# The last expert's up projection ahead of three of its neighbour's down pieces; list slots by position; weights spread by GpSimd; lists read back by a gather

## What is computed

```python
logits = xt @ w_router + b_router
top_vals, top_idx = lax.top_k(logits, 4)            # 32 experts, 4 of them for a token
top_gates = softmax(top_vals)
# for each expert e, on its rows xb:
gate = minimum(xb @ w_gate[e] + b_gate[e], 7)
up = clip(xb @ w_up[e] + b_up[e], -7, 7)
y = (gate * sigmoid(1.702 * gate) * (up + 1)) @ w_down[e] + b_down[e]
out[token] += top_gates[token, e] * y               # summed over the token's experts
```

## Time and profile before

| | |
|---|---|
| three runs, median (lowest to highest) | 1674.03 us (1672.72 to 1676.4) |
| the profiled execution | 1675.01 us |
| its span in the trace | 1673.7 us |
| TensorE busy | 1609.6 us (96%) |
| VectorE busy | 1351.4 us (81%) |
| ScalarE busy | 1194.3 us (71%) |
| GpSimd busy | 239.6 us (14%) |
| chain that ended last | PE 76%, DVE 13%, ACT 6%, issue 3%, DMA 1% |

### The profile page before, as it was taken

One profiled execution on the slowest core, in us unless ns is written; L12 is line 12 of the kernel. 1 busy time (PEld: TensorE's weight loads), 2 busy tenths in 40 slices (PEclk: granted clock), 3 DMA queues, 4 the chain that ended last, 5 costly groups with the idle time before them and its releaser, 6 DMA issues.

```text
span 1673.7 us, 19532 instructions
## 1 busy us (share of the span) xinstructions
PE 1609.6 (96%) x7495; PEld 1301.5 (78%) x7495; DVE 1351.4 (81%) x1059; ACT 1194.3 (71%) x932; POOL 239.6 (14%) x170
## 2 busy tenths in 40 slices
PE   8999979999999999999999999999999999999998
PEld 6877867777877877877877877877776887788886
DVE  4576689999999999999999999999997535864343
ACT  5354358888888888888898898898894366763232
POOL 2502037131121121121111111112010000000000
PEclk9999989999999999999999999999999999999999
DMA  8412379999999999999999999999994512114311
GB/s 295 136 51 76 124 278 334 406 404 415 414 406 417 411 409 415 408 413 408 410 416 403 411 412 406 410 412 399 403 395 134 188 64 76 51 57 176 101 63 51
DMA packets 97343, 487.86 MB, mean 291 GB/s; under 512 B 14645, under 2 KB 16365, under 8 KB 48096
## 3 DMA queue, kind: packets, MB, share of 16 engines
q1 hardware_dynamic: 82848, 463.69, 69.4%
q0 software_dynamic: 10480, 18.17, 4.2%
q10 hardware_dynamic: 3920, 4.72, 0.8%
HBM read 478.00 MB, written 25.08 MB: 301 GB/s over the span
## 4 chain that ended last, share of the span: by engine, by line
PE 76%; DVE 13%; ACT 6%; issue 3%; DMA 1%; DVEq 0%; ACTq 0%
PE PS L574 68%; ACT WH L1129 5%; DVE WL L1503 4%; DVE low L1503 4%; PE PS L835 3%; PE PS L1050 1%; DVE eu L1865 1%; DVE eu L1870 1%; PE PS L849 1%; PE PS L606 1%; DVE hl L1856 1%; DMA h2d<-HV 1%; PE PS L1064 1%; PE PS L705 0%; PE PS L1043 0%
## 5 line engine op out<-in xcount | busy, mean ns | idle before, releaser
L1129 ACT ACTIVATE WH<-land 128x2048 fp32r<-128x2048 f32 x210 | 396.5, 1912 | 134.6 <-PE PS L574 134.0
L1129 ACT ACTIVATE WH<-ring 128x2048 fp32r<-128x2048 f32 x216 | 407.7, 1912 | 87.3 <-PE PS L574 82.9
L1503 DVE TENSOR_TENSOR low<-ring,WH 128x2048 fp32r<-128x2048 f32 x194 | 437.1, 2287 | 19.5 <-ACT WH L1129 18.6
L1503 DVE TENSOR_TENSOR WL<-land,WH 128x2048 fp32r<-128x2048 f32 x190 | 427.5, 2287 | 20.4 <-ACT WH L1129 19.6
L2223 POOL DMA_INDIRECT accd<-ys,lists x28 | 60.2, 2149 | 742.6 <-ACT ys L1337 734.0
L574 PE MATMUL PS<-WH,xh 128*128 128x512 f32 x512 | 161.0, 396 | 4.1 <-DVE low L1503 1.9
L574 PE MATMUL PS<-WH,hh 128*128 128x512 f32 x512 | 147.4, 389 | 0.0
L574 PE MATMUL PS<-WH,xs 128*128 128x512 f32 x512 | 144.4, 405 | 1.8 <-DVE xs L1854 1.8
L574 PE MATMUL PS<-WH,xl 128*128 128x512 f32 x512 | 137.2, 390 | 0.0
L574 PEld LDWEIGHTS PS<-WH,xs 128*128 128x128 f32 x512 | 98.1, 195 | 22.0 <-issue 2.2
L574 PE MATMUL PS<-h,WH 128*128 128x512 f32 x288 | 113.4, 394 | 0.0
(11 more groups left out here) (443 smaller groups left out, 2975.8 us busy)
## 6 DMA issues: line engine op xcount, KB each, us to landing
land<-in_w_up_dram SPq DMA_DIRECT2D x71, 1024.0 KB, 9.8
ring<-in_w_down_dram SPq DMA_DIRECT2D x71, 1024.0 KB, 10.6
ring<-in_w_gate_dram SPq DMA_DIRECT2D x66, 1024.0 KB, 10.7
land<-in_w_gate_dram SPq DMA_DIRECT2D x62, 1024.0 KB, 11.2
ring<-in_w_up_dram SPq DMA_DIRECT2D x57, 1024.0 KB, 10.2
land<-in_w_down_dram SPq DMA_DIRECT2D x57, 1024.0 KB, 10.8
ring<-in_w_in_dram SPq DMA_DIRECT2D x19, 1024.0 KB, 13.0
land<-in_w_in_dram SPq DMA_DIRECT2D x13, 1024.0 KB, 5.4
```

The lines of the kernel that those rows point to most:

```text
L1129: A.activation(WH[buf[n]], lands[spot[n]], ACT.Copy).then_inc(s_hi, 1)
L1503: V.tensor_tensor(WLn[n], lands[spot[n]], WH[buf[n]].bitcast(F32), SUB).then_inc(s_lo, 1)
```

## The change

- *Last expert.* In stage 31 the order of pieces is `d0 g6 g7 d1 d2 d3` at the end in place of `d0 g6 d1 g7 d2 d3`. The fold of expert 31's up part moves from behind d3 to behind d1, the clamp and product to ahead of the third low half, the transposes from behind d3 to behind d2; their result goes into `xh` instead of `hh`. The bias half and the matmuls of `tensor_hold` between them go; the bias half stands in the join, whose order changes.
- *Slots.* A slot is now position times 32 plus expert, made by one step from the position `P1`; the bit steps go, and two short steps stand in the routing. The lists are read back by one indirect gather, with row numbers `laid`.
- *Weights.* `spread_out` goes; `gpsimd_spread`, three element-wise steps on GpSimd, stands between the first and the second gather there. `vector_further_count` moves behind `vector_last`.
- *Expert 0 and 1.* ScalarE's and VectorE's copies of expert 1's rows move by one piece; `scalar_out(0)` moves from g0 to g4 of stage 2.
- *Warm-up.* One, one and six more matmuls behind the routing's parts, and eleven instead of eight ahead of expert 0.

```diff
@@ -249,4 +251,2 @@
     pvk = reg("pvk", [128, 4, E, K], F32, 17)
-    ri = reg("ri", [128, 4, E], I32, 50)
-    bits = [reg(f"bits{i}", [128, 4, E], I32, (48, 48.5, 50.5, 51)[i]) for i in range(4)]
     WH += [reg(f"WH{3 + i}", [128, 4, 512], F32R, 53.5 + 16 * i) for i in range(2)]
@@ -342,3 +342,4 @@
             return [("d", p) for p in range(4)]
-        return [(a[0], int(a[1])) for a in "g0 g1 g2 g3 g4 g5 d0 g6 d1 g7 d2 d3".split()]
+        row = "g0 g1 g2 g3 g4 g5 d0 g6 d1 g7 d2 d3" if e + 1 < E else "g0 g1 g2 g3 g4 g5 d0 g6 g7 d1 d2 d3"
+        return [(a[0], int(a[1])) for a in row.split()]
 
@@ -477,9 +478,2 @@
 
-    def spread_out(o, v):
-
-        V.tensor_tensor(e2, eq, v.unsqueeze(2).broadcast_to([128, 4, E, K]), MUL).then_inc(dv.sem, dv.one())
-        V.wait_ge(dv.sem, dv.n)
-        return V.tensor_reduce(o, e2, AX, ADD)
-
-
     s_land = s_ring + [s_gpre, s_glog, s_gt, s_wz, s_wgh]
@@ -806,3 +800,5 @@
         tensor_route(1)
+        tensor_stay_warm(1)
         turn2(2)
+        tensor_stay_warm(1)
         turn2(3)
@@ -810,2 +806,4 @@
         tensor_route(3)
+        P.wait_ge(s_tall, 16)
+        tensor_stay_warm(6)
         P.wait_ge(s_m16, 1)
@@ -938,3 +936,3 @@
                 P.wait_ge(s_spk, 1)
-        rows_by_columns(n_d[e, p], p, 4, hh, hl, 0 if p else t_mid[e] + 1, small(e)).then_inc(s_mm, 1)
+        rows_by_columns(n_d[e, p], p, 4, hh if e + 1 < E else xh, hl, 0 if p else t_mid[e] + 1, small(e)).then_inc(s_mm, 1)
         if p == 0 and small(e + 1):
@@ -944,5 +942,7 @@
             tensor_turn_rows(e + 2)
-        if p == 3 and small(e + 1):
+        if p == (3 if e + 2 < E else 1) and small(e + 1):
             P.wait_ge(s_low, fold["up", e + 1])
             tensor_fold(2, eul).then_inc(s_fold, 1)
+        if p == 2 and e + 2 == E:
+            tensor_turn_mid(E - 1)
 
@@ -951,3 +951,3 @@
         tensor_index(0, 7)
-        tensor_stay_warm(8)
+        tensor_stay_warm(11)
         tensor_turn_rows(0)
@@ -957,6 +957,2 @@
                 tensor_down_bias(0)
-                tensor_hold(6, 3)
-                tensor_turn_mid(E - 1)
-                tensor_down_bias(1, (0,))
-                tensor_hold(3, 3)
             for what, p in items(e):
@@ -975,8 +971,2 @@
 
-    def tensor_hold(bank, times):
-        P.wait_ge(s_lo, n_d[E - 1, 0] + 1)
-        P.wait_ge(s_tl, t_rows[E - 1] + 1)
-        for _ in range(times):
-            mm(PS[:, bank, :], foldw, WH[buf[n_d[E - 1, 0]]][:, 0], True, True)
-
     def tensor_last(j, part, end):
@@ -996,3 +986,3 @@
     def tensor_join():
-        tensor_down_bias(1, (1,))
+        tensor_down_bias(1, (0,))
         P.wait_ge(s_last, 3)
@@ -1000,5 +990,6 @@
         tensor_last(0, yh, False)
-        tensor_last(1, yh, False)
+        tensor_down_bias(1, (1,))
         P.wait_ge(s_last, 4)
         tensor_last(0, yl, True)
+        tensor_last(1, yh, False)
         tensor_last(1, yl, True)
@@ -1345,3 +1336,2 @@
                 scalar_out(E - 2)
-                scalar_turn8(t_mid[E - 1], hh, E - 1)
             for what, p in items(e):
@@ -1353,6 +1343,12 @@
                     scalar_rows(e + 1)
-                if (what, p) == ("d", 2) and small(e):
+                if (what, p) == ("d", 2 if e + 1 < E else 1) and small(e):
                     scalar_up_low(e)
+                if (e, what, p) == (E - 1, "d", 3):
+                    scalar_turn8(t_mid[E - 1], xh, E - 1)
+                if (what, p) == ("g", 7) and e == 0:
+                    scalar_rows(1)
+                    A.wait_ge(s_spt, 1)
+                    A.activation(GtT, PS[0:32, 5, :].rearrange("p (j t) -> p j t", j=4), ACT.Copy).then_inc(s_spk, 1)
                 high(ahead(n_g[e, p] if what == "g" else n_d[e - 1, p]))
-                if (what, p) == ("g", 2 if small(e) else 0) and e >= 2:
+                if (what, p) == ("g", 2 if small(e) else 4 if e == 2 else 0) and e >= 2:
                     scalar_out(e - 2)
@@ -1362,6 +1358,2 @@
                     scalar_gate(e)
-                if (what, p) == ("g", 7) and e == 0:
-                    scalar_rows(1)
-                    A.wait_ge(s_spt, 1)
-                    A.activation(GtT, PS[0:32, 5, :].rearrange("p (j t) -> p j t", j=4), ACT.Copy).then_inc(s_spk, 1)
         high(second + 1)
@@ -1714,2 +1706,5 @@
                     low(first)
+                    V.tensor_scalar(chosen[:, :, :, 0], C[:, TOKK:TOKK + 16].rearrange("p (j k) -> p j k", j=4), -1.0, None, ADD).then_inc(dv.sem, dv.one())
+                    V.wait_ge(dv.sem, dv.n)
+                    V.tensor_scalar(chosen[:, :, :, 0], chosen[:, :, :, 0], 2, None, ALU.arith_shift_right)
         invert(8, 7)
@@ -1799,6 +1794,4 @@
         step = lambda o: o.then_inc(dv.sem, dv.one())
-        step(V.tensor_scalar(ri, P1, -1.0, None, ADD))
         V.wait_ge(s_ek, 1)
         step(V.reciprocal(sm, sm))
-        step(V.tensor_scalar(chosen[:, :, :, 0], C[:, TOKK:TOKK + 16].rearrange("p (j k) -> p j k", j=4), -1.0, None, ADD))
         step(V.tensor_tensor(past, P1, late[:, OVT:OVT + 96].rearrange("p (e j) -> p e j", j=3)[:, :, 0].unsqueeze(1).broadcast_to([128, 4, E]), ALU.is_gt))
@@ -1806,11 +1799,6 @@
         V.tensor_tensor(GK, GK, sm.unsqueeze(2).broadcast_to([128, 4, 4]), MUL).then_inc(s_gk, 1)
-        step(V.tensor_scalar(bits[0], ri, 7, None, ALU.bitwise_and))
-        step(V.tensor_scalar(bits[1], ri, 8, None, ALU.bitwise_and))
-        step(V.tensor_scalar(bits[2], ri, 48, None, ALU.bitwise_and))
-        step(V.tensor_scalar(bits[3], ri, 64, None, ALU.bitwise_and))
         step(V.scalar_tensor_tensor(pv, past, 8 * BIG, C[:, IOTA:IOTA + E].unsqueeze(1).broadcast_to([128, 4, E]), MUL, ADD))
         V.wait_ge(dv.sem, dv.n)
-        for b, times in ((0, 128.0), (1, 256.0), (2, 2.0), (3, 16.0)):
-            step(V.scalar_tensor_tensor(pv, bits[b], times, pv, MUL, ADD))
-            V.wait_ge(dv.sem, dv.n)
+        step(V.scalar_tensor_tensor(pv, P1, 1.0 * E, pv, MUL, ADD))
+        V.wait_ge(dv.sem, dv.n)
         step(V.tensor_tensor(pvk, eqr, pv.unsqueeze(3).broadcast_to([128, 4, E, K]), MUL))
@@ -1818,3 +1806,2 @@
         step(V.tensor_reduce(slots, pvk.rearrange("p j e k -> p j k e"), AX, ADD))
-        step(V.tensor_scalar(chosen[:, :, :, 0], chosen[:, :, :, 0], 2, None, ALU.arith_shift_right))
         V.wait_ge(s_gk, 1)
@@ -1822,3 +1809,3 @@
         V.wait_ge(dv.sem, dv.n)
-        V.tensor_copy(sloti, slots).then_inc(s_sig, 1)
+        V.tensor_scalar(sloti, slots, -1.0 * E, None, ADD).then_inc(s_sig, 1)
 
@@ -1898,14 +1885,14 @@
         low(first + NX - 1)
-        spread_out(Gt, GK).then_inc(s_sp, 1)
-        vector_further_count()
         for e in range(E + 1):
             if e == E:
-                vector_turn8(t_mid[E - 1], hh, hl, E - 1)
                 vector_last()
+                vector_further_count()
             for what, p in items(e):
-                if (what, p) == (("d", 1) if e else ("g", 7)) and e + 1 < E:
+                if (what, p) == (("d", 1) if e else ("g", 6)) and e + 1 < E:
                     vector_turn8(t_rows[e + 1], xs if small(e + 1) else xh, xl, e + 1)
-                if (e, what, p) == (E - 1, "d", 3):
+                if (e, what, p) == (E - 1, "d", 2):
                     vector_up(E - 1)
                     vector_glu(E - 1)
+                if (e, what, p) == (E - 1, "d", 3):
+                    vector_turn8(t_mid[E - 1], xh, hl, E - 1)
                 low(ahead(n_g[e, p] if what == "g" else n_d[e - 1, p]))
@@ -2205,5 +2192,14 @@
 
+    def gpsimd_spread():
+        G.wait_ge(s_gk, 1)
+        G.tensor_tensor(e2, eq, GK.unsqueeze(2).broadcast_to([128, 4, E, K]), MUL).then_inc(po.sem, po.one())
+        G.wait_ge(po.sem, po.n)
+        G.tensor_tensor(e2[:, :, :, 0:2], e2[:, :, :, 0:2], e2[:, :, :, 2:4], ADD).then_inc(po.sem, po.one())
+        G.wait_ge(po.sem, po.n)
+        G.tensor_tensor(Gt, e2[:, :, :, 0], e2[:, :, :, 1], ADD).then_inc(s_sp, 1)
+
     def gpsimd_lists():
         G.wait_ge(s_small, 400)
-        G.dma_start(lists.rearrange("p s a -> p (s a)"), listd.rearrange("(p s) a -> p (s a)", s=E)).then_inc(s_small, 16)
+        G.indirect_dma_start(lists.rearrange("p s a -> p (s a)"), None, listd.rearrange("(p s) a -> p (s a)", s=E),
+                             bass.IndirectOffsetOnAxis(laid, 0), bounds_check=127, oob_is_err=False).then_inc(s_small, 16)
         G.wait_ge(s_small, 416)
@@ -2248,6 +2244,9 @@
         gpsimd_gather(1)
+        gpsimd_spread()
         gpsimd_gather(2)
         G.wait_ge(s_sig, 3)
+        G.tensor_copy(laid, C[:, LAID:LAID + 1]).then_inc(po.sem, po.one())
         G.wait_ge(s_small, 144)
         gpsimd_list(0, 16)
+        G.wait_ge(po.sem, po.n)
         gpsimd_lists()
```

(4 more changed lines are left out.)

## The result

Over 20 runs each the changed kernel took **1679.15 us** (1671.39 to 1683.14), the kernel before 1674.89 us (1672.26 to 1676.69): ratio **1.0018**, 95% interval 1.001 to 1.0026, slower by 4.3 us by the medians (3.0 us by the ratio). The forecast of 1678.8 us is 0.35 us off, and inside its range. But its parts are not right: in the profiles the start gained where a loss was forecast, the end lost more, and the join, forecast at nothing, lost most.

The account below looks back on a forecast made before the run. TensorE and VectorE bound the middle, so only the ends could move the time, VectorE bounding the start. Profiled 1675.01 us plus 2.0, 1.1 and 1.7 gave 1679.8, less 1.0 for the median: 1678.8, range 1671.2 to 1681.8.

Parts of the forecast that it names:

- Start: Start of the experts, up to expert 0's GLU product: ends 2.0 us later, bounds -4.1 to +3.0.
- the cost of the spread on GpSimd: Start: GpSimd's last spread step waits for VectorE's row of five low halves; weights known at 254.2 instead of 248.0.
- Rival A: Start: GpSimd's third step slips in between low halves; about -3.5 us at the GLU product; chance 0.31 in three forms.
- The warm-ups: Added TensorE matmuls ahead of the experts: up to 1.5 us later there, nothing in the sum while VectorE is the bound.
- Slots and counts: VectorE, start: shorter slots gain 1.8 us; spread and counts leaving gain 2.30, the counts moving about 1 us at no cost.
- Last expert: TensorE: expert 31's down part starts 1.1 us later, bounds -1 to +2; a slow clock adds 1.7 us.
- The wait: TensorE runs dry for 3.3 us ahead of the last expert's transposes; expert 31's down part starts 1.1 us later.
- The half clock: TensorE behind the last expert's wait: clock at 0.50 over 3 to 4 us of work, +1.7 us; 0 if it holds.
- The join: The order of bias and list steps in the join only fills a gap of 0.3; nothing in the sum.

Follow-up runs that it names:

- spread late: The changed kernel with GpSimd's three spread steps behind the second gather instead of ahead of it; 1682.93 us, ratio 1.0048.
- spread on VectorE: The changed kernel with last expert and join as before, and the weights' spread back on VectorE, none on GpSimd; 1672.70 us, ratio 0.9988.
- wait filled: The changed kernel with twelve unused matmuls in TensorE's wait ahead of the last expert's transposes; 1672.74 us, ratio 0.9996.
- end alone: The kernel before with only the last expert's new order and the new join; 1677.28 us, ratio 1.0023.
- old join: The changed kernel with the join's order as before; 1676.10 us, ratio 1.0008.
- GLU earlier: The changed kernel with the last expert's clamp and product one low half earlier on VectorE; 1670.63 us, ratio 0.9973.
- join filled: GLU earlier with five unused matmuls ahead of the join's first transposes; 1669.76 us, ratio 0.9975.

## Why the prediction was right in its sum and wrong in its steps

- **Start, forecast +2.0, measured -2.4** at the GLU product. The step that failed is the cost of the spread on GpSimd, in two places. It was put behind low half +4 by adding the old duration of one step to the old time of the gather. The gather came 0.87 us earlier, and, what decides, the steps held up VectorE's `pvk` by 1.64 us and with it +4, so they were all over by then. And a step that does meet the row waits for one low half, not for all of them (spread late). Rival A, the open seam, had the sign of the start right (-3.5 forecast for it, -2.4 measured, of which 0.87 is the earlier gather), but in the changed kernel no step needed a seam. The warm-ups, at nothing in the sum, stay unsettled.
- **The Trainium skill's rule** (SBUF — State Buffer, Who interferes with whom): contention between a two-input VectorE instruction and a GpSimd instruction that reads SBUF is in the traces here, as `pvk` at 2.33 instead of 0.69 us. The same section says that issue order decides who blocks; in the records `pvk` starts 0.70 us ahead of GpSimd's step and is the one that is held. As it lasts 0.69 us alone, it would have been over just when that step starts; so these records don't show which of the two was issued first, and neither bear the rule out nor refute it.
- **Slots and counts, forecast 1.8 us and (of the 2.30) some 1.0**: right. With the spread on VectorE the GLU product ends 29.13 us after the first gather starts (268.95 and 239.82), before 31.87: 2.74 us.
- **Last expert, forecast +1.1 and +1.7, measured +3.74** from fold to down. The wait (3.3 forecast, 3.06 measured) and its own price (1.1 forecast, 1.02 with the wait filled) are right. The half clock was mis-sized for this profile: 2.7 us instead of 1.7, as it covered the transposes and the whole piece behind them, up to about 1260. It is not one size: behind the same wait it cost 2.7 and 2.6 in the two profiles of the changed kernel, 1.6 in those of the end alone and of spread late, and nothing in that of the old join.
- **The join, forecast at nothing, measured +4.17** in the profiled execution. This term was missing: the prediction asked of the join's new order only what gap it fills, and not what TensorE's clock does there. It was at half for 7 us in the kernel before and for 17 in the changed one. By the mean clocks a time this long comes in nine of 20 runs. Of the kernels with the wait unfilled, those with the new join have runs above 1679 us (ten of 20 and three of three of the changed kernel, five of twelve of the end alone, four of six of spread late, whose start is 2.8 us later), the old join none of eleven. Without the wait (GLU earlier, and with the join filled) one run of 20, 1676.3 us, lies more than 4 us above its kernel's median.
- **The sum** was right by luck: the two errors, -4.4 us in the start and +5.1 in end and join of the profile, nearly cancel; the middle gave back another 0.8 us of the start's gain, and the median, with half of its runs free of the long half clock, lies below the profile and could have lain at either group's.

What stays open is why the half clock in the join lasts 17 us in some runs, and what in the new order brings it. From 1265 to 1300 us the mean granted clock was 0.90, 7 us of half clock, in all five profiles with the old order of the join; with the new order it was 0.76 twice, 0.95 twice (3.4 us), 0.90 once (GLU earlier) and 1.00 twice (wait filled, join filled). The 7 us began, in all six, during a wait of 1.03 to 1.12 us ahead of the join's first transposes or within 1.5 us behind it; the 3.4 and the 17 us began at about 1274, with no wait of over 0.29 us in the 10 us ahead of them. So the new order makes the half clock there vary, from nothing to 17 us, rather than always lengthen it.

## What to carry to other kernels

Moving a step to an idle engine need not take its time off the busy one: here the busy engine's own next step took 1.64 us longer, so measure that step too. Ahead of a move that makes the bounding engine wait once, even by 3 us, ask what its clock does behind it; here the wait itself cost 1.0 us and the half clock right behind it up to 2.7. Where runs fall into groups, look at each group before trusting a median: a forecast can meet it by luck. The wait was on another engine's order of steps, and one swap there (product ahead of a low half) turned a loss of 0.2% into a gain of 0.3%.

## What was not expected of the hardware

A GpSimd step with two inputs in SBUF got in at the seam between back-to-back low halves, each time after one of them (2.22, 2.54 and 2.34 us), while the copy of 32x2 elements stood for three. And the granted clock stayed at 0.50 for 17 us with TensorE busy in every 4-us stretch (4.00 of 4.00 us), where it was at 0.50 for 7 us in the kernel before and at 1.00 throughout with the wait or the join filled.
